# GpSimd's drains replaced by a semaphore, and one group of pooled sums spread over five slots

## The reference

```python
h = rms_norm(x, norm1); proj = h @ w_in
q, k, v, z, xbc, dt, xp = split(proj)
o_sb   = stick_breaking_attention(q, [past_k, k], [past_v, v])   # 2048 past tokens in pages of 128
y_ssd  = rms_norm((ssd(conv(xbc), dt) + d_skip * xs) * silu(z))
y_pool = (mean of the last 2, 4, 8 or 16 rows of xp, minus xp) @ pool_w * pool_scale   # 4 groups
x = x + concat(o_sb, y_ssd, y_pool) @ w_out
x = x + (silu(conv3(rms_norm(x) @ w_gate)) * (rms_norm(x) @ w_up)) @ w_down
```

## Time and profile before

| | us |
|---|---|
| median of 3 runs | 3318.3 (3315.88 to 3321.15) |
| profiled execution, its own time | 3309.06 |
| span of the profiled execution | 3307.4 |
| busy in it: PE / DVE / ACT / POOL | 3200.8 / 1897.9 / 1346.8 / 409.5 |
| granted clock of TensorE, mean | 0.99 |

### The profile page before, as it was taken

How to read it: one execution, slowest core, us unless ns; L and a number is a source line. 1 busy time by engine, 2 the same in 40 slices (tenths; PEclk the granted TensorE clock), 3 DMA queues, 4 the chain that set the end, 5 groups by cost and what they waited for, 6 DMA issues and landing times.

```text
span 3307.4 us, 62432 instructions
## 1 busy us (share of the span) xinstructions
PE 3200.8 (97%) x23776; PEld 3015.1 (91%) x23776; DVE 1897.9 (57%) x3339; ACT 1346.8 (41%) x1663; POOL 409.5 (12%) x513
## 2 busy tenths in 40 slices
PE   7999899999999999999999998989999999999998
PEld 7999566799999999999999985659999999999998
DVE  4574655466654665366756655464666546654664
ACT  4553565444432333333335545563444333333332
POOL 0000654220000000000200026541100000000002
PEclk9999899999999999999999999999999999999999
DMA  6433699744444444444544347995444444444443
GB/s 188 141 127 103 209 307 300 242 148 145 152 143 151 152 149 146 153 147 140 157 138 140 129 133 226 322 301 182 149 152 146 148 153 147 145 154 143 149 149 101
DMA packets 469101, 554.42 MB, mean 168 GB/s; under 512 B 20635, under 2 KB 414444, under 8 KB 468788
## 3 DMA queue, kind: packets, MB, share of 16 engines
q1 hardware_dynamic: 440275, 466.93, 43.7%
q0 software_dynamic: 26192, 84.73, 7.9%
q10 hardware_dynamic: 2449, 0.27, 0.1%
HBM read 535.50 MB, written 16.38 MB: 167 GB/s over the span
## 4 chain that ended last, share of the span: by engine, by line
PE 90%; ACT 2%; issue 2%; DMA 2%; POOLq 1%; DVE 1%; POOL 1%; ACTq 0%; PEld 0%; DVEq 0%; PEldq 0%; SPq 0%
PE ps L1141 26%; PE ps L1143 26%; PE ps L1142 26%; PE ps L1366 2%; PE ps L1410 2%; PE ps L1378 1%; PE ps L1528 1%; PE ps L1518 1%; DMA vring<-in_cache_v 1%; PE ps L1512 1%; PE ps L1455 1%; POOLq L610 0%; ACT wz L949 0%; DMA raw<-in_w_out 0%; PE ps L1392 0%
## 5 line engine op out<-in xcount | busy, mean ns | idle before, releaser
L1638 DVE TENSOR_TENSOR wl<-raw,wh 128x1024 fp32r<-128x1024 f32 (+1 forms) x736 | 903.1, 1236 | 992.8 <-ACT wh L760 985.0
L760 ACT ACTIVATE wh<-raw 128x1024 fp32r<-128x1024 f32 (+1 forms) x736 | 764.7, 1041 | 1601.1 <-PE ps L1143 1592.5
L1141 PE MATMUL ps<-fh,wh 128*128 128x320 f32 x2816 | 870.6, 309 | 0.0
L1143 PE MATMUL ps<-fh,wl 128*128 128x320 f32 x2816 | 870.1, 309 | 0.0
L1142 PE MATMUL ps<-fl,wh 128*128 128x320 f32 x2816 | 870.1, 309 | 0.0
L1141 PEld LDWEIGHTS ps<-fh,wh 128*128 128x128 f32 x2816 | 528.5, 188 | 0.2
L1142 PEld LDWEIGHTS ps<-fl,wh 128*128 128x128 f32 x2816 | 528.5, 188 | 0.2
L1143 PEld LDWEIGHTS ps<-fh,wl 128*128 128x128 f32 x2816 | 528.5, 188 | 0.0
L1141 PE MATMUL ps<-hh,wh 128*128 128x320 f32 x1376 | 428.1, 311 | 5.5 <-DVE wl L1638 4.5
L1141 PE MATMUL ps<-ah,wh 128*128 128x320 f32 x1376 | 427.2, 310 | 0.0
L1143 PE MATMUL ps<-hh,wl 128*128 128x320 f32 x1376 | 425.8, 309 | 0.0
(11 more groups left out here) (405 smaller groups left out, 3661.7 us busy)
## 6 DMA issues: line engine op xcount, KB each, us to landing
raw<-in_w_gate SPq DMA_DIRECT2D x88, 1024.0 KB, 5.0
raw<-in_w_up SPq DMA_DIRECT2D x88, 1024.0 KB, 5.0
raw<-in_w_in SPq DMA_DIRECT2D x72, 1024.0 KB, 5.0
kring<-in_cache_k SPq DMA_DIRECT2D x256, 256.0 KB, 4.0
vring<-in_cache_v POOLq DMA_DIRECT2D x256, 256.0 KB, 4.5
raw<-in_w_down SPq DMA_DIRECT2D x64, 1024.0 KB, 5.4
raw<-in_w_out SPq DMA_DIRECT2D x32, 1024.0 KB, 6.6
raw<-in_w_down SPq DMA_DIRECT2D x32, 768.0 KB, 4.6
```

The costliest lines, as they stand in the source:

```text
L760: act.activation(wh[:, s % 2, half, :], raw[:, s, half, :], ACT.Copy).then_inc(hi_done, 1)
L1141: pe.matmul(out, wh[:, s % 2, kk, w], hi(row), start=first, stop=False)
L1143: mm = pe.matmul(out, wl[:, s % 2, kk, w], hi(row), start=False, stop=last)
L1638: dve.tensor_tensor(wl[:, s % 2, half, :], raw[:, s, half, :], wh[:, s % 2, half, :].bitcast(F32), ALU.subtract).then_inc(lo_done, 1)
```

## The change

A new semaphore `pool_step` counts GpSimd's own steps. In `pooled` and `gate` each drain is replaced by an increment on the instruction before it and a wait of GpSimd for the next count (`settled`). The two means share one increment, on the second. The squares keep their drains. `pooled` is cut into `pooled_sum(g, n)`, one doubling sum with its wait, and `pooled_mean(g)`, the rest. Groups 0, 1 and 2 run them in one go in slots 1, 6 and 9 as before. Group 3, which stood in slot 20, runs its four sums in slots 22, 23, 24 and 25, and its means in slot 26, each behind that slot's `value_in`. The order of the sums and the arithmetic are the same; `p1` and `p2` take the same turns.

```diff
--- before.py
+++ after.py
@@ -14,6 +14,7 @@
 from concourse import mybir
 from collections import namedtuple
 from contextlib import ExitStack
+from itertools import count
 
 F32 = mybir.dt.float32
 F32R = mybir.dt.float32r
@@ -359,7 +360,7 @@
         conv_stored = sem("conv_stored")
         tail_stored, ftail_T, ftail_out = sem("tail_stored"), sem("ftail_T"), sem("ftail_out")
 
-        passed = sem("passed")
+        passed, pool_step = sem("passed"), sem("pool_step")
 
         block = ctx.enter_context(nc.Block())
 
@@ -546,6 +547,12 @@
             pool.dma_start(con[:, 0:K_NEG], a["con"][:, 0:K_NEG]).then_inc(ident_loaded, 16)
             pool.dma_start(con[:, K_NEG:], a["con"][:, K_NEG:]).then_inc(con_loaded, 16)
 
+            steps = count(1)
+
+            def settled():
+
+                pool.wait_ge(pool_step, next(steps))
+
             def square(buf, g, last=KT // 2 - 1):
 
                 two = x[:, 2 * g:2 * g + 2, :]
@@ -599,25 +606,27 @@
 
                 xps = xp[:, :, SEQ + PH:].rearrange("p g (b t) -> p g b t", b=NB)
 
-                def pooled(g):
-
-                    win = WINS[g]
-                    src, w, bufs = xp[:, g, :], 1, [p1, p2]
-                    while w < win:
-                        dst = bufs[0][:]
-                        bufs.reverse()
-                        pool.tensor_tensor(dst[:, 2 * w - 1:], src[:, 2 * w - 1:], src[:, w - 1:XPL - w], ALU.add)
-                        pool.drain()
-                        src, w = dst, 2 * w
+                def pooled_sum(g, n):
+
+                    w = 2 ** n
+                    src = (p2, p1)[n % 2][:] if n else xp[:, g, :]
+                    dst = (p1, p2)[n % 2][:]
+                    pool.tensor_tensor(dst[:, 2 * w - 1:], src[:, 2 * w - 1:], src[:, w - 1:XPL - w], ALU.add
+                                       ).then_inc(pool_step, 1)
+                    settled()
+
+                def pooled_mean(g):
+
+                    win, src = WINS[g], (p1, p2)[g % 2][:]
                     news = pdiff[:, g, SEQ:TOK].rearrange("p (b t) -> p b t", b=NB)
                     pool.tensor_scalar(pdiff[:, g, 0:SEQ], src[:, PH:PH + SEQ], 1.0 / win, None, ALU.mult)
                     pool.tensor_scalar(news, src[:, SEQ + PH:].rearrange("p (b t) -> p b t", b=NB)[:, :, PH:], 1.0 / win,
-                                       None, ALU.mult)
-                    pool.drain()
+                                       None, ALU.mult).then_inc(pool_step, 1)
+                    settled()
 
                     pool.tensor_tensor(pdiff[:, g, 0:16], src[:, PH:PH + 16], con[:, K_CNT + 16 * g:K_CNT + 16 * g + 16],
-                                       ALU.mult)
-                    pool.drain()
+                                       ALU.mult).then_inc(pool_step, 1)
+                    settled()
                     pool.tensor_tensor(pdiff[:, g, 0:SEQ], pdiff[:, g, 0:SEQ], xp[:, g, PH:PH + SEQ], ALU.subtract)
                     pool.tensor_tensor(news, news, xps[:, g, :, PH:], ALU.subtract).then_inc(p_diff, 1)
 
@@ -652,10 +661,10 @@
                     cols = slice(blk * P, (blk + 1) * P)
                     read(pool, l, "y", blk, 2)
                     read(pool, l, "y", blk, 3)
-                    pool.tensor_tensor(y[:, :, cols], y[:, :, cols], z[:, :, cols], ALU.mult)
-                    pool.drain()
-                    pool.tensor_tensor(z[:, :, cols], y[:, :, cols], y[:, :, cols], ALU.mult)
-                    pool.drain()
+                    pool.tensor_tensor(y[:, :, cols], y[:, :, cols], z[:, :, cols], ALU.mult).then_inc(pool_step, 1)
+                    settled()
+                    pool.tensor_tensor(z[:, :, cols], y[:, :, cols], y[:, :, cols], ALU.mult).then_inc(pool_step, 1)
+                    settled()
                     pool.tensor_tensor(z[:, 0:4, cols], z[:, 0:4, cols], z[:, 4:8, cols], ALU.add).then_inc(y_sq, 1)
 
                 def state_decay(i):
@@ -690,8 +699,15 @@
                         slot = 8 * qn + k
                         if 2 <= qn <= CHUNKS:
                             value_in(qn - 1, k)
-                        if slot in (1, 6, 9, 20):
-                            pooled((1, 6, 9, 20).index(slot))
+                        for g, at_ in enumerate((1, 6, 9)):
+                            if slot == at_:
+                                for n in range(g + 1):
+                                    pooled_sum(g, n)
+                                pooled_mean(g)
+                        if 22 <= slot < 26:
+                            pooled_sum(3, slot - 22)
+                        if slot == 26:
+                            pooled_mean(3)
                         for blk in range(3):
                             if slot == SLOT["cum", blk] + 2:
                                 weighted_x(blk)
```

## The result

The changed kernel takes 3298.0 us (median of 14 runs, 3287.4 to 3315.3) where the kernel before, timed beside it, takes 3318.8 us (14 runs, 3306.0 to 3322.5). The ratio is 0.9942, with a 95% interval of 0.9929 to 0.9954: 15 to 24 us faster, the middle at 19.2. The forecast was 3294.3 us and a gain of 24.0 us.

What follows compares the result with a forecast made beforehand. GpSimd, a whole ring late through long drains, was taken to stall TensorE, itself busy 97%. Gains of 10.6 us in layer 0 and 13.4 in layer 1, 24.0 together, took the median from 3318.3 to 3294.3 us; range 3286 to 3311.

Steps and rivals of the forecast that it cites:

- The long drains: GpSimd's pooled sums and gate: drains wait for its own transfers in flight, leaving gaps of 2.54 to 4.61 us.
- The price of a wait on itself: GpSimd's new semaphore waits: 0.1 us each, the same as a cheap drain.
- Rival 2: GpSimd's new wait trails its loads as the drain did; some 5 us slower in each layer, 3328 us; chance 0.06.
- The fourth group: Slots 20 to 26: slot 21's load at 372.7, 2.3 us per sum slot, weighted product ending near 391.
- Collisions with VectorE: Layer 1: GpSimd's arithmetic and VectorE's slow each other; 1.0 us taken off the 4.5 us gain, 3.5 kept.
- No slack in layer 1: Weighted product ends at 2020.6, TensorE's L1487 needs it at 2020.7; a further GpSimd microsecond costs TensorE one.
- rival 1: Gain only in part, from more VectorE meetings or layer 1's missing slack: 8 to 16 us, 3302 to 3310; chance 0.13.
- What TensorE gets back: TensorE's gain in the mixing stages: 10.6 us in layer 0 and 13.4 us in layer 1, 24.0 us together.
- the stall and its clock: TensorE's value-page waits go, 9.2 us in layer 0, 7.3 in layer 1, plus 2.4 us of slow clock each.
- the term for catching up: 1.0 us taken off in each layer because ScalarE and VectorE had used TensorE's stall to catch up.
- the tails' wait: Layer 1, TensorE's 3.96 us wait: 1.0 us left standing; with 1.7 us of slow clock, 4.7 us gained.
- rival 3: Stall given back in TensorE's slots 30 to 34, waiting for ScalarE, VectorE or transfers; gain under 6.6 us; chance 0.09.

Runs made afterwards that it cites:

- e2: The kernel before with the fourth pooled group in five pieces over slots 22 to 26, drains kept: 3324.8 us against 3315.1.
- g3: The kernel before, all drains kept, without the value loads after each layer's first eight: 3291.6 us against 3317.0, one run.
- e1: The changed kernel with the fourth pooled group whole in slot 20, semaphore kept: 3294.9 us against 3315.1 before, ratio 0.9947.
- e6: The changed kernel with two TensorE pooling products moved from slots 29 and 39 to 39 and 45: 3296.8 us, ratio 0.9944 to before.
- f1: The changed kernel with drains again behind the gate's first two products: 3300.9 us against 3313.7 before, ratio 0.9962.
- f4: The kernel before with the semaphore in the fourth pooled group alone, whole in slot 20: 3308.2 us, ratio 0.9981.
- f2: The changed kernel with the fourth group whole in slot 20 and drains behind the gate's first two products: 3306.3 us, ratio 0.9968 to before.
- g4: e2 without the value loads after each layer's first eight: 3294.0 us against 3317.0 for the kernel before, one run.

## Why the prediction was right, and where it was off

**The long drains: right.** That they wait for GpSimd's own transfers was read from two pairs of rows; e2 and g3 show it in either direction, with loads a landing for each drain, without them 0.14 us. The reading was too narrow in one place: the gate's drain was put down to the value load alone, and the tails' store ahead of it is enough. The Trainium skill, page PSUM — Partial Sum Buffer, section Engine vs sequencer instructions, says that a drain waits for the engine to go fully idle and advises to put an increment on the producing instruction; the traces agree, and show that for GpSimd "fully idle" takes in its transfers.

**The price of a wait on itself: right.** 0.1 us was taken, 0.08 to 0.10 us is measured wherever a new wait stands. Rival 2, that the increment trails the loads, falls with it: the gate's wait passed at 368.09 with a load in flight to 370.2, and in the five slots, where each sum stands right behind a load, the next load follows after 1.2 us idle and not after a landing.

**The fourth group: the direction right, two sizes off, its worth overrated.** Slot 21's load was put at 372.7 and went out at 373.53. A sum slot was put at 2.3 us and takes 2.7 (377.39 to 380.13): with a sum between two loads 1.2 us pass idle ahead of the load, not the 0.6 us of loads in a row. So the weighted product ends at 393.5 and not near 391, and TensorE reaches the product that needs it at 397.11, later than the 395 expected, with 3.6 us to spare. What failed is that the prediction never asked what the semaphore gives without the move. By its own numbers slot 21's load would have come at 388.69-2.4-3.2-2.6 = 380.5 and its page near 385, against a need at 382.4, a short stall; e1's load went out at 379.44 and there was no stall.

**Collisions with VectorE: a deduction for nothing.** 1.0 us was taken off. The weighted product and VectorE's scan in the changed kernel (count, ns min/median/max; before: the earlier trace rows):

```profile
L639 POOL TENSOR_TENSOR xw<-xtok,tk x6: 1892/1913/1917, 343.3 to 2045.3; 128x1024 f32<-128x1024 f32 x4, 64x1024 f32<-64x1024 f32 x2
...
L2045 DVE TENSOR_TENSOR_SCAN sq<-rz,sq,lq x24: 1275/1283/2326, 368.7 to 2220.8; 128x512 f32<-128x512 f32 x24
```

The worst case of the one fell from 3257 to 1917 ns and of the other from 2979 to 2326, and GpSimd's busy time did not grow, though single instructions still ran long (the gate's second product 2.70 us in layer 1, 1.89 in layer 0). Whether the rule of the Trainium skill that was weighed there (page SBUF — State Buffer, section SBUF: two separate sides, the exclusive lock of the shared ports) is at work in the 2326 ns, no run here shows; that the change pays more for it than the kernel before, the busy time denies. GpSimd therefore gained more in layer 1: the tails' store went out 1980.88-1944.67 = 36.2 us into the layer instead of 1991.96-1950.93 = 41.0, 4.8 us earlier where 3.5 were counted, and of the 3.96 us wait nothing was left where 1.0 was.

**"No slack in layer 1": the product's time was right, the need for it wrong.** The weighted product ended 2012.74+1.92-1944.67 = 70.0 us into the layer, forecast were 2020.6-1950.93 = 69.7. Two errors of it cancelled: slot 18's load came earlier than counted (1985.66, 41.0 us into the layer, 42.7 forecast), and from there to the product's end it took 29.0 us instead of 27. TensorE wanted it at 72.8 us instead of the 69.8 forecast, so it had 2.8 us to spare, and rival 1's wait for GpSimd did not come.

**What TensorE gets back: the stall and its clock were right, the term for catching up was mis-sized, and one loss was not in the sum.** TensorE's slots can be set side by side, each counted from its key page's transposition to that of the layer's slot 0 (L1366 before, L1382 after). Gains in us:

| part | layer 0, forecast | measured | layer 1, forecast | measured |
|---|---|---|---|---|
| slots 0 to 26, in layer 1 0 to 20 | 0 | -0.9 | 0 | -1.6 |
| layer 0: wait of 0.90 us in slot 27; layer 1: the tails' wait and its clock, slots 21 and 22 | 0.9 | 1.0 | 4.7 | 5.6 |
| value stall of slot 29 and its clock, slots 29 and 30 | 10.7 | 10.7 | 9.7 | 9.7 |
| catching up, slots 31 to 33 | -1.0 | -1.6 | -1.0 | -3.2 |
| sum | 10.6 | 9.2 | 13.4 | 10.4 |

So the two estimates of the slow clock behind a value stall, 2.4 us each, came out to 0.1 us, and the tails' part was 0.9 better than forecast. Catching up cost more than the 1.0 us a layer that was allowed for ScalarE and VectorE. In layer 0 it is 0.97+0.90 us less the 0.36 that stood there before. In layer 1 it is 1.90 us, 2.05-1.16 = 0.9 for the slow product behind it, and slow ones next to that (the granted clock was 0.89 from 2010 to 2020). This is rival 3's mechanism at a small part of its size. e6 shows that moving one of the two waits away brings the other.

The loss ahead of the stall, 0.9 and 1.6 us, stands in slots 13 to 16 in both layers. In layer 1, before, then after:

```profile
1980.58 0.66 PE L1466 MATMUL ps<-seg,xtok 128*64 128x128 f32 x8 [1.82 <-DVE y L2096]
```

```profile
1974.81 1.12 PE L1482 MATMUL ps<-seg,xtok 128*64 128x128 f32 x8 [1.81 <-DVE y L2112]
```

The wait for VectorE is the same; the product behind it is slower, and the granted clock as a mean from 1970 to 1980 was 0.83 after and 1.00 before (layer 0, 350 to 360: 0.84 and 1.00). f1's layer 1 has the wait and keeps 1.00. So this is no fixed price of the change; what decides it stays open.

**From the profile to the median: right.** The forecast carried the gain of one execution over to a median. The gain by medians, 20.8 us, and by stretches, 19.6 us, agree within what a single execution can tell.

## What to carry to other kernels

On a GpSimd queue that issues transfers and computes between them, a drain between two dependent instructions costs 0.1 to 0.3 us while no transfer is in flight and what is left of the landing (1 to 5 us here) when one is, and what then comes late is the next transfer; an increment on the producer and a wait of the same engine cost 0.1 us in either case. Look in the trace for idle time between two instructions of one engine that ends just behind a landing. Spreading work over a queue's slots buys cover against lateness elsewhere, and does harm while each piece still carries a drain.

## What was not expected of the chip

**The granted clock took back in one execution most of what the change gave.** The stretch after the inter-chunk product of layer 1 (L1503), up to the stage behind that layer's mixing, took 243.8 us in the profiled execution before and 258.8 us after, though the work is the same. Windows over most of it, before, then after (the number behind the five engines is the granted clock):

```profile
2040.00:2280.00 240.00, 219.40 (x2294) 161.31 (x2282) 128.50 (x210) 134.20 (x218) 99.27 (x136) 0.99 0.89 290
```

```profile
2024.00:2276.00 252.00, 230.98 (x2238) 169.86 (x2234) 127.18 (x208) 133.24 (x217) 99.13 (x135) 0.92 0.85 275
```

TensorE was busy 91 to 92% in both. In the other kernels' profiles the same stretch took 241 to 254 us. Among those with all their loads it was 244 to 246 in the three with a stall of over 4 us in layer 1 (before, e2, f4), 251 in f2 with its 3.71, and 248 to 259 in the six without one; without the loads, and without a stall, 241 and 252 (g3, g4). With one execution of each, this doesn't show whether a removed stall is in part paid back behind it, but it is not ruled out. The 14 runs of the changed kernel order themselves nearly by the mean clock, from 3287.4 us at 0.994 to 3315.3 at 0.983. What lowers the clock in a stretch without a long stall stays open; no run here was made for it.
